# One of three attention stages rebuilt: two heads a step in the halves of TensorE's array, V stationary, branches summed in PSUM

## The chip, the cores and the metric

The kernel runs on one core of one Trainium2 chip. The metric is the device time of one launch in microseconds; smaller is better.

## The reference

Three transformer-like blocks in a row over 512 tokens of width 1024, all in float32. The third block holds the part that matters here, an attention of 16 heads of 64 with four groups of keys and values (four heads share one), in three branches whose outputs are summed with gates:

```python
# q: 16 heads; k_cmp/v_cmp, k_slc/v_slc, k_win/v_win: 4 groups; gates: sigmoid, 3 per head
y = g0 * attend(q, k_cmp, v_cmp) + g1 * attend(q, k_slc, v_slc) + g2 * attend(q, k_win, v_win)
mixed = merge[0] * (y_diff @ w_proj_diff) + merge[1] * (y @ w_proj_nsa)
```

The compressed branch has 31 keys, 32 in the kernel. At 512 tokens the selected and the window branch are both plain causal attention over all earlier keys, each with its own keys and values. Each row of scores gets its own maximum, exponential and sum.

## The kernel before

The program is a list of 43 stages, run by all engines in the same order, with a barrier between stages (`barrier`, L276: every engine drains and adds one to a semaphore, and waits until all four have). A stage marked `AHEAD` lets TensorE skip that wait and go on. Weights stream in through two slots on SyncE's queue for the whole program; most stages are matmuls in three fp32r parts over them (L148 to L186). The stages here, in order:

`to_fm` (L1395, planned at L2075) turns queries and keys with TensorE transposes to feature-major form; ScalarE copies them out of PSUM, the queries to `QF` (16 heads, two in the 128 partitions of each of 8 slices), each half of the keys to the lower 64 rows of `KF` (L1412). GpSimd fills the upper 64 rows of `KF` and of `QZN` with zeros (L1788).

`cattn` (L1678 to L1774) computes the gates `GT` and the compressed branch: scores with 64-row matmuls (L1686), softmax scaled by its gate, transposes (L1695), values with `PTC` stationary and `VBD` moving (L1703), copies to `ON` (L1772).

`nsa` (L1793 to L1819) is the two causal branches, with the helpers that the other attention stages use too: `attn_pe`, `attn_act`, `attn_dve` (L1097 to L1154). A loop over four groups has 32 steps each: one head, one branch and one block of 128 queries a step. The step's scores are one matmul with the zero-padded queries stationary and (block + 1) x 128 keys moving (L1094) and a mask matmul in bf16 (L1095). VectorE takes the negated maximum (L1165), ScalarE the exponential with the row sum (L1160). Three steps later TensorE transposes the weights (L1112) and ScalarE copies them (L1136); one step after that TensorE multiplies them with V, the turned weights stationary, V moving 64 columns (L1121). After four steps VectorE divides by the sum, applies the gate and adds to `ON` (L1808 to L1817). Scores have four PSUM banks, turned weights two, outputs two. A group starts with ScalarE copying four heads to `QZN` (L1264).

`split_fm` (L1286) turns `ON` to feature-major form and splits it in two fp32r parts, `YNH` (L1300) and `YNL` (L1306). `merge` (L1830 to L1875) projects both attentions; its first matmul of a pass waits for `mg.free`, which VectorE raises at the start of its part of the stage (L1856).

Engines run their instructions in order. Nothing but the text of the functions sets the order in the attention stages.

Of the kernel before, what the change touches and what calls it, by code (L numbers as in the profile page):

```python
# [23 lines left out]
ALU = mybir.AluOpType  # L24
# [3 lines left out]
P = 128  # L28
# [15 lines left out]
NSA_G = 4  # L44
# [6 lines left out]
def build(nc, A, out):  # L51
# [1104 lines left out]
    def one_softmax(act, dve, PBx):  # L1156
# [393 lines left out]
    ON = a_("ON", 0, [P, NC_, DM])  # L1550
    nq, nkv = turn(left_s, left=8), turn(left_s, left=12)


# [120 lines left out]
    PTC = a_("PTC", 72, [P, 2, SEQ])  # L1674
    GFM = PTC[:, 0, :]
    ca = sems("ca", "gate sig mask sc m ex p tr pt o od")

    def cattn_pe(pe):  # L1678
        narrow_pe(pe, nr[2], 6, SW[1], 0, 48, GFM).then_inc(ca.gate, 1)
        pe.wait_ge(ca.sig, 1)  # L1680
        for g in range(NSA_G):
            for r in range(2):
                half = slice(r * HD, (r + 1) * HD)
                for k in range(2 * NC_):
                    qb, j = divmod(k, 2)
# [3 lines left out]
        for g in range(NSA_G + 1):
            if g < NSA_G:  # L1690
                pe.wait_ge(ca.p, g + 1)
                if g >= 2:
                    pe.wait_ge(ca.pt, g - 1)
                for qb in range(NC_):
                    last = pe.transpose(PS[:, g % 2, qb * P:(qb + 1) * P], T3[:, g, qb * P:(qb + 1) * P], IDF[:, :])  # L1695
                last.then_inc(ca.tr, 1)
            if g:
                q = g - 1
                pe.wait_ge(ca.pt, q + 1)
                if q >= 2:  # L1700
                    pe.wait_ge(ca.od, q - 1)
                for qb in range(NC_):
                    last = pe.matmul(PS[:, 2 + 2 * (q % 2) + qb // 2, (qb % 2) * 256:(qb % 2) * 256 + 256],  # L1703
                                     PTC[:, q % 2, qb * P:(qb + 1) * P], VBD[:, q, :], start=True, stop=True)
                last.then_inc(ca.o, 1)

    def cattn_act(act):
        act.wait_ge(ca.gate, 1)
        act.activation(GT[:, :, :], PS[:, 7, 0:192].rearrange("p (c k) -> p c k", c=NC_), ACT.Sigmoid)
        act.drain().then_inc(ca.sig, 1)  # L1710
        for g in range(NSA_G):
            act.wait_ge(ca.m, g + 1)
            act.activation(SC[g], SC[g], ACT.Exp).then_inc(ca.ex, 1)
        for g in range(NSA_G):
            act.wait_ge(ca.tr, g + 1)
            if g >= 2:
                act.wait_ge(ca.o, g - 1)
            act.activation(PTC[:, g % 2, :], PS[:, g % 2, :], ACT.Copy).then_inc(ca.pt, 1)
# [10 lines left out]
    def cattn_dve(dve):  # L1729
# [39 lines left out]
        for g in range(NSA_G):  # L1769
            dve.wait_ge(ca.o, g + 1)  # L1770
            for b in range(2):
                dve.tensor_copy(ON[:, 2 * b:2 * b + 2, g * 256:(g + 1) * 256],  # L1772
                                PS[:, 2 + 2 * (g % 2) + b, :].rearrange("p (a k) -> p a k", a=2))
            dve.drain().then_inc(ca.od, 1)  # L1774

    QZN = a_("QZN", 76, [P, HPG, SEQ])
    PTN = a_("PTN", 72, [P, 2, SEQ])
    OTMP = a_("OTMP", 84, [P, NC_, HD])  # L1780
    NSTEP = HPG * 2 * NC_
    na = attn_turn(NSA_G, NSTEP, 4)

    def pn(t, a, b):

        return T3[:, t % NP, a:b]

    def zero_rows(pool):  # L1788

        for T in (KF[0], KF[1], QZN):  # L1790
            pool.memset(T[HD:P, :, :], 0.0)

    def nsa_pe(pe):  # L1793
        attn_pe(pe, na, NSA_G, NSTEP, 4,
                lambda g, t: scores_pe(pe, t % 4, QZN[:, t // 8, (t % 4) * P:(t % 4 + 1) * P],
                                       lambda n: flat(KF[t // 4 % 2][:, ds(g, 1), 0:n]), t % 4),
                lambda k, b: pn(k, b * P, (b + 1) * P), PTN,
                lambda g, k, b: T3[:, b, ds(768 + 512 * (k // 4 % 2) + HD * g, HD)], (na.ex, na.at.ex + 4 + 1), HD)

    def nsa_act(act):  # L1800
        exps, _ = one_softmax(act, None, pn)
        attn_act(act, na, NSA_G, NSTEP, 4, lambda g: head_queries(act, QZN, QF, g), exps, PTN)

    def nsa_dve(dve):
        def output(g, q):
            hh, branch = q // 2, q % 2
            inv, rw = (RW[:, 8 * (q % 2) + r:8 * (q % 2) + r + 4] for r in (0, 4))
            dve.reciprocal(inv, RS[:, 4 * (q % 4):4 * (q % 4) + 4])  # L1808
            dve.drain()
            dve.tensor_tensor(rw.unsqueeze(2), inv.unsqueeze(2),  # L1810
                              GT[:, :, ds(12 * g + 3 * hh + 1 + branch, 1)], ALU.mult)
            dve.drain()
            dve.tensor_tensor(OTMP[:, :, :], PS[:, 6 + q % 2, 0:256].rearrange("p (c d) -> p c d", c=NC_),
                              rw.unsqueeze(2).to_broadcast([P, NC_, HD]), ALU.mult)
            dve.drain()
            o = ON[:, :, ds(g * 256 + hh * HD, HD)]
            return dve.tensor_tensor(o, o, OTMP[:, :, :], ALU.add)  # L1817
# [201 lines left out]
    def stages(e, kind):  # L2019

        fns = STAGES[kind]
        for k, fn in enumerate(fns):
            if fn is not None:
# [148 lines left out]
```

## Time and profile before

| | |
|---|---|
| median of 3 runs | 3137.61 us (3129.13 to 3139.46) |
| the profiled execution | span 3135.7 us, first to last instruction |
| TensorE busy | 2773.3 us, 88% |
| VectorE, ScalarE, GpSimd busy | 1427.0, 1149.6, 35.4 us |
| TensorE's mean granted clock | 0.933 of 2.4 GHz |

Times are microseconds from the span's start. PE is TensorE's matmuls, PEld its weight loads, DVE is VectorE, ACT ScalarE, POOL GpSimd. PEclk is the granted clock as a share of 2.4 GHz; 0.50 is 1.2 GHz. Ends of matmuls are modelled, so starts are the firmer numbers.

### The profile page before, as it was taken

The page shows a single profiled execution, that of the slowest core. Times are in us where ns is not written, and L with a number is a line of the kernel's source. Part 1 is how long each engine was busy: PE and PEld are TensorE (multiplying, and loading weights), DVE is VectorE, ACT ScalarE, POOL GpSimd, SP SyncE. Part 2 cuts the span into 40 slices and gives each one's busy share as a digit, 9 for nine tenths or more (in the row PEclk, how much of TensorE's full clock was granted, in tenths as well). Part 3 has the DMA queues.
Part 4 walks back from the last instruction along what each step waited for, and adds up shares of the span by engine and source line. Part 5 has one row for each costly group of instructions (what it writes and reads, how often), then busy time and mean ns, then how long its engine had stood idle before and what let it go on. Part 6 is the DMA issues. An engine that isn't in the chain of part 4 may idle for free. (4 is left out here: it accounts for less than half of the span.)

```text
span 3135.7 us, 37199 instructions
## 1 busy us (share of the span) xinstructions
PE 2773.3 (88%) x12589; PEld 2174.5 (69%) x12589; DVE 1427.0 (46%) x2122; ACT 1149.6 (37%) x1965; POOL 35.4 (1%) x86
## 2 busy tenths in 40 slices
PE   7994879899997989889999796887489999899998
PEld 5872658588784867668877575676467788677776
DVE  3465232677524223367732476664444433252332
ACT  2241231455313346255521424433256633242231
POOL 0000000000001000000000000000100000000000
PEclk8997779999998999999999898998599999999999
DMA  3330002133221310123322121131000033222332
GB/s 110 96 95 6 27 27 94 54 94 100 94 94 34 94 54 0 54 67 94 100 94 87 44 88 34 45 96 54 4 1 0 0 94 97 78 74 94 87 94 81
DMA packets 270183, 206.36 MB, mean 66 GB/s; under 512 B 12004, under 2 KB 225681, under 8 KB 270113
## 3 DMA queue, kind: packets, MB, share of 16 engines
q1 hardware_dynamic: 258384, 197.16, 20.6%
q10 hardware_dynamic: 11729, 8.28, 0.8%
q8 instruction: 42, 0.69, 0.1%
q14 instruction: 28, 0.23, 0.0%
HBM read 203.28 MB, written 2.10 MB: 65 GB/s over the span
## 5 line engine op out<-in xcount | busy, mean ns | idle before, releaser
L146 DVE TENSOR_TENSOR WL<-RAW,WH 128x1024 fp32r<-128x1024 f32 x370 | 453.2, 1225 | 1021.7 <-ACT WH L141 1016.7
L141 ACT ACTIVATE WH<-RAW 128x1024 fp32r<-128x1024 f32 x370 | 391.7, 1059 | 1073.8 <-PE PS L155 864.7
L153 PE MATMUL PS<-XH,WH 128*128 128x512 f32 x1504 | 595.0, 396 | 56.8 <-DVE XL L593 28.3
L154 PE MATMUL PS<-XL,WH 128*128 128x512 f32 x1504 | 590.5, 393 | 0.0
L155 PE MATMUL PS<-XH,WL 128*128 128x512 f32 x1504 | 590.0, 392 | 0.0
L153 PEld LDWEIGHTS PS<-XH,WH 128*128 128x128 f32 x1504 | 285.2, 190 | 131.8 <-issue 49.0
L155 PEld LDWEIGHTS PS<-XH,WL 128*128 128x128 f32 x1504 | 285.4, 190 | 60.2
L154 PEld LDWEIGHTS PS<-XL,WH 128*128 128x128 f32 x1504 | 285.8, 190 | 57.7
L150 PE MATMUL PS<-WH,XH 128*128 128x512 f32 x480 | 199.0, 414 | 18.4 <-DVE WL L146 8.5
L151 PE MATMUL PS<-WH,XL 128*128 128x512 f32 x480 | 196.0, 408 | 0.0
L152 PE MATMUL PS<-WL,XH 128*128 128x512 f32 x480 | 195.3, 407 | 0.0
L1165 DVE TENSOR_REDUCE NM<-PS 128x1 f32<-128x128 f32 x192 | 93.4, 490 | 149.6 <-PE PS L1095 149.5
L153 PE MATMUL PS<-FH,WH 128*128 (+1 forms) x352 | 139.1, 395 | 3.3 <-ACT UP L691 3.3
L155 PE MATMUL PS<-FH,WL 128*128 (+1 forms) x352 | 138.9, 395 | 0.0
L154 PE MATMUL PS<-FL,WH 128*128 (+1 forms) x352 | 138.9, 395 | 0.0
L150 PEld LDWEIGHTS PS<-WH,XH 128*128 128x128 f32 x480 | 96.5, 201 | 43.6 <-DVE WL L146 11.8
L152 PEld LDWEIGHTS PS<-WL,XH 128*128 128x128 f32 x480 | 95.5, 199 | 21.2
L151 PEld LDWEIGHTS PS<-WH,XL 128*128 128x128 f32 x480 | 96.0, 200 | 20.2
L153 PE MATMUL PS<-MH,WH 128*128 (+1 forms) x256 | 101.3, 396 | 3.3 <-ACT RL L1906 3.3
L155 PE MATMUL PS<-MH,WL 128*128 (+1 forms) x256 | 101.1, 395 | 0.0
L154 PE MATMUL PS<-ML,WH 128*128 (+1 forms) x256 | 101.1, 395 | 0.0
L1121 PE MATMUL PS<-T,PTN 128*128 x640 | 87.0, 267 | 1.9 <-ACT PTN L1136 0.7
(431 smaller groups left out, 4059.6 us busy)
## 6 DMA issues: line engine op xcount, KB each, us to landing
RAW<-in_ffn_w_up SPq DMA_DIRECT2D x88, 512.0 KB, 3.7
RAW<-in_w_in SPq DMA_DIRECT2D x60, 512.0 KB, 3.5
RAW<-in_sc_ssm_w_in SPq DMA_DIRECT2D x44, 512.0 KB, 3.6
RAW<-in_ffn_w_down SPq DMA_DIRECT2D x44, 512.0 KB, 3.5
RAW<-in_w_mlp_up SPq DMA_DIRECT2D x32, 512.0 KB, 4.0
RAW<-in_w_mlp_down SPq DMA_DIRECT2D x32, 512.0 KB, 3.6
RAW<-in_fox_w_in SPq DMA_DIRECT2D x24, 512.0 KB, 3.7
RAW<-in_sc_ssm_w_out SPq DMA_DIRECT2D x16, 512.0 KB, 3.6
```

What stands on the lines that cost most here:

```text
L141: act.activation(WH[:, slot, :], RAW[:, slot, :], ACT.Copy).then_inc(hi_ready, 1)
L146: dve.tensor_tensor(WL[:, slot, :], RAW[:, slot, :], WH[:, slot, :], ALU.subtract).then_inc(lo_ready, 1)
L150: pe.matmul(o, ah, wh, start=first, stop=False)
L151: pe.matmul(o, al, wh, start=False, stop=False)
L152: return pe.matmul(o, ah, wl, start=False, stop=last)
L153: pe.matmul(o, wh, ah, start=first, stop=False)
L154: pe.matmul(o, wh, al, start=False, stop=False)
L155: return pe.matmul(o, wl, ah, start=False, stop=last)
L1121: last = pe.matmul(PS[:, 6 + k // NC_ % 2, o], PTx[:, k % 2, b * P:(b + 1) * P], value(i, k, b), start=b == 0, stop=b == k % 4)
L1165: return dve.tensor_reduce(NM[:, t % 4:t % 4 + 1], PS[:, t % 4, 0:w], AX, ALU.max, negate=True)
```

## The change

The attention stage gets helpers of its own. A step `t` of 16 is one pair of heads in one branch, with all four blocks of queries; heads are read in place from `QF`, partitions 0 to 63 and 64 to 127, and the keys are kept twice, once in each half of the partitions. Scores come in three parts (`SUBS`): block 3; blocks 2 and 0; block 1. They have two pairs of PSUM banks. The weights are normalised and gated by GpSimd before they are turned, in five chunks through two banks. Values have V stationary (64 columns) and the turned weights moving, so the output is feature-major already; the two branches and the compressed one add up in one PSUM bank. A stage `ysplit` then only splits `QF` in two parts.

```diff
+    SUBS = (((3, 0),), ((2, 0), (0, 384)), ((1, 0),))
+    CHUNKS = (((0, 0, 0),), ((0, 1, 0), (0, 3, 384)), ((1, 0, 0),), ((1, 1, 0), (1, 3, 384)),
+              ((0, 2, 0), (1, 2, 256)))
...
+    def pair_scores_pe(pe, s, t, sub, query, key, bias=None):
+        i = 3 * t + sub
+        if i >= 2:
+            pe.wait_ge(s.ex, s.at.ex + i - 1)
+        banks = [2 * (i % 2) + hh for hh in range(2)]
+        for hh in range(2):
+            for k, (qb, c0) in enumerate(SUBS[sub]):
+                d = c0 + qb * P
+                pe.matmul(PS[:, banks[hh], d:d + P], IDB[:, :], MROW[:, :], start=k == 0, stop=False,
+                          skip_group_check=True)
+        for qb, c0 in SUBS[sub]:
+            n = (qb + 1) * P
...
+            for hh in range(2):
+                last = pe.matmul(PS[:, banks[hh], c0:c0 + n], query(t, hh, qb), key(t, hh, n), start=False,
+                                 stop=True, skip_group_check=True)
+        last.then_inc(s.sc, 1)
+
+    def pair_turn_pe(pe, s, t, chunk, Px):
+        j = 5 * t + chunk
+        if chunk == 0:
+            pe.wait_ge(s.nr, s.at.nr + 3 * t + 3)
+        if j >= 2:
+            before = chunk - 2 if chunk >= 2 else chunk + 3
+            done = t if chunk >= 2 else t - 1
+            if before in (0, 2):
+                pe.wait_ge(s.pa, s.at.pa + 2 * done + before // 2 + 1)
+            else:
+                pe.wait_ge(s.pd, s.at.pd + 3 * done + {1: 1, 3: 2, 4: 3}[before])
...
+    def pair_values_pe(pe, s, t, o, opens, PTx, value):
+        pe.wait_ge(s.pa, s.at.pa + 2 * t + 2)
+        pe.wait_ge(s.pd, s.at.pd + 3 * t + 3)
+        for b in range(NC_):
+            for hh in range(2):
+                last = pe.matmul(PS[64 * hh:64 * hh + 64, 6 + o % 2, b * P:SEQ], value(t, hh, b), pt_of(PTx, hh, b),
+                                 start=opens and b == 0, stop=b == NC_ - 1, skip_group_check=True)
+        last.then_inc(s.pv, 1)
+
+    def pair_pe(pe, s, n, Px, PTx, query, key, value, bias=None, first_values=None, per_out=1):
+        for t in range(n + 2):
+            if t < n:
+                pe.wait_ge(s.qk, s.at.qk + t // per_out + 1)
+                pair_scores_pe(pe, s, t, 0, query, key, bias)
+            if t >= 2:
+                k = t - 2
+                o = k // per_out
+                if k % per_out == 0 and o >= 2:
+                    pe.wait_ge(s.od, s.at.od + o - 1)
+                if k % per_out == 0 and first_values is not None:
+                    first_values(pe, o)
+                pair_values_pe(pe, s, k, o, k % per_out == 0 and first_values is None, PTx, value)
+            if t < n:
+                pair_scores_pe(pe, s, t, 1, query, key, bias)
+            if 1 <= t <= n:
+                for chunk in range(3):
+                    pair_turn_pe(pe, s, t - 1, chunk, Px)
+            if t < n:
+                pair_scores_pe(pe, s, t, 2, query, key, bias)
+            if 1 <= t <= n:
+                for chunk in range(3, 5):
+                    pair_turn_pe(pe, s, t - 1, chunk, Px)
...
+    def pair_act(act, s, n, Px, PTx, output, per_out=1):
+        for t in range(n + 2):
+            if t < n:
+                pair_exps_act(act, s, t, 0, Px)
+                pair_exps_act(act, s, t, 1, Px)
+            if t >= 2 and (t - 2) % per_out == per_out - 1:
+                act.wait_ge(s.pv, s.at.pv + t - 1)
+                output((t - 2) // per_out).then_inc(s.oa, 1)
+            if 1 <= t <= n:
+                for chunk in (0, 2):
+                    act.activation(*pair_copy(act, s, t - 1, chunk, PTx), ACT.Copy).then_inc(s.pa, 1)
+            if t < n:
+                pair_exps_act(act, s, t, 2, Px)
...
+    def pair_dve(dve, s, n, PTx, output, per_out=1):
+        for t in range(n + 2):
+            if t < n:
+                pair_maxima_dve(dve, s, t, 0)
+            if 1 <= t <= n:
+                pair_weights_dve(dve, s, t - 1, 2)
+            if t < n:
+                pair_maxima_dve(dve, s, t, 1)
+                pair_weights_dve(dve, s, t, 0)
+            if t >= 2 and (t - 2) % per_out == per_out - 1:
+                o = (t - 2) // per_out
+                dve.wait_ge(s.oa, s.at.oa + o + 1)
+                output(o).then_inc(s.od, 1)
+            if 1 <= t <= n:
+                dve.tensor_copy(*pair_copy(dve, s, t - 1, 1, PTx)).then_inc(s.pd, 1)
+            if t < n:
+                pair_maxima_dve(dve, s, t, 2)
+                pair_weights_dve(dve, s, t, 1)
+            if 1 <= t <= n:
+                for chunk in (3, 4):
+                    dve.tensor_copy(*pair_copy(dve, s, t - 1, chunk, PTx)).then_inc(s.pd, 1)
+
+    def pair_pool(pool, s, n, Px, gate=None):
...
+                for qb, _ in SUBS[sub]:
+                    for hh in range(2):
+                        col = 8 * (t % 2) + NMCOL[qb] + hh
+                        p = Px[:, t % 2, hh, POFF[qb]:POFF[qb] + (qb + 1) * P]
+                        pool.tensor_scalar(p, p, RW[:, col:col + 1], 1.0 if gate is None else gate(t, hh, qb),
+                                           ALU.mult, ALU.mult)
+                pool.drain().then_inc(s.nr, 1)
...
                     for h, d in enumerate(dst):
-                        last = act.activation(d[0:HD, :], PS[h * HD:(h + 1) * HD, k % 4, :], ACT.Copy)
+                        for to in range(2):
+                            last = act.activation(d[to * HD:(to + 1) * HD, :], PS[h * HD:(h + 1) * HD, k % 4, :], ACT.Copy)
...
     def cattn_pool(pool):
+        for b in range(2):
+            pool.tensor_copy(VN[b][:, :, :], T3[:, :, 768 + 512 * b:1024 + 512 * b])
...
+        def compressed(pe, o):
+            pe.matmul(PS[:, 6 + o % 2, :], VBD[:, o // 2, (o % 2) * P:(o % 2 + 1) * P], PTC[:, o // 2, :],
+                      start=True, stop=False, skip_group_check=True)
+        pair_pe(pe, na, 2 * NPAIR, PN, PTN, query, key, value, None, compressed, 2)
...
+    def ysplit_act(act):
+        for j in range(KT):
+            act.activation(YNH[:, j, :], QF[:, j, :], ACT.Copy).then_inc(ny.hi, 1)
+
+    def ysplit_dve(dve):
+        for j in range(KT):
+            dve.wait_ge(ny.hi, j + 1)
+            dve.tensor_tensor(YNL[:, j, :], QF[:, j, :], YNH[:, j, :], ALU.subtract).then_inc(ny.lo, 1)
...
                 ah, al = ((YDH, YDL), (YNH, YNL), (XH, XL), (XH, XL))[u % 4]
+                if isinstance(i, int) and u == 1:
+                    pe.wait_ge(ny.lo, KT)
                 unit_fm(pe, first["merge"], 8, i, u, PS[:, u, :], ah, al)
-        loop(pe, "merge", body)
+        loop(pe, "merge", body, peel=1)
...
-              pool_too=zero_rows),
+              ),
         (cattn_pe, cattn_act, cattn_dve, cattn_pool),
-        (nsa_pe, nsa_act, nsa_dve, None),
-        split_fm(ON, YNH, YNL),
+        (nsa_pe, nsa_act, nsa_dve, nsa_pool),
+        (None, ysplit_act, ysplit_dve, None, AHEAD),
```

Not shown: `cattn` loses its values (L1703), its copies to `ON` (L1772) and the waits between them; the old bodies of `nsa_pe`, `nsa_act`, `nsa_dve` and `zero_rows` go; tiles move in SBUF. `pair_weights_dve` is one reciprocal of the sums for each part of the scores. The output copy of `pair_act` writes `QF`; that of `pair_dve` is a drain. The other two attention stages are as they were.

## Rows read from the trace of the kernel before

**Rows 1.** The page's first line.

```profile
span 3135.7 us, 37199 instructions
```

**Rows 2.** Stretches of attention and split; busy time (instructions) by engine, PEclk, DMA, GB/s.

```profile
2290.00:2492.40 202.40, 191.95 (x1344) 151.83 (x1344) 96.20 (x256) 136.94 (x400) 0.00 (x0) 0.97 0.00 0
2492.40:2500.40 8.00, 5.73 (x33) 5.26 (x34) 5.16 (x9) 4.67 (x9) 0.00 (x0) 0.79 0.01 2
```

**Rows 3.** Timeline of one head and branch; start, duration, engine, line, count, idle before.

```profile
2353.06 0.44 PE L1094 MATMUL PS<-KSF,QZN 128*128 x2
...
2355.81 0.61 PE L1112 MATMUL PS<-IDF,T 128*128 128x128 f32 x4
...
2356.26 0.78 PE L1121 MATMUL PS<-T,PTN 128*128 x6
...
2356.87 1.08 PE L1094 MATMUL PS<-KSF,QZN 128*128 x2
...
2357.79 0.22 PE L1095 MATMUL PS<-MROW,IDB 128*128 128x128 bf16 x1
...
2357.96 1.00 PE L1121 MATMUL PS<-T,PTN 128*128 x8
2358.04 0.69 DVE L1165 TENSOR_REDUCE NM<-PS 128x1 f32<-128x512 f32 x1 [1.47 <-PE PS L1095]
...
2358.80 0.44 PE L1094 MATMUL PS<-KWF,QZN 128*128 x2
...
2359.07 0.22 PE L1095 MATMUL PS<-MROW,IDB 128*128 128x128 bf16 x1
```

**Rows 4.** Groups of 2226 to 2290 us, the 64-row matmuls; busy, mean ns.

```profile
L1686 PE MATMUL PS<-KCF,QF 64*128 64x32 f32 x128 | 20.7, 389 | 1.8 <-ACTq L1710 1.8
```

**Rows 5.** Groups of the attention stage by form; busy, mean ns, idle before.

```profile
L1136 ACT ACTIVATE PTN<-PS 128x512 f32<-128x512 f32 x32 | 19.1, 597 | 11.5 <-PE PS L1112 11.5
L1160 ACT ACTIVATE T<-PS,NM 128x384 f32<-128x384 f32 x32 | 18.4, 575 | 2.8 <-DVE NM L1165 2.8
L1165 DVE TENSOR_REDUCE NM<-PS 128x1 f32<-128x384 f32 x32 | 17.8, 557 | 14.6 <-PE PS L1095 14.6
...
L1160 ACT ACTIVATE T<-PS,NM 128x128 f32<-128x128 f32 x32 | 11.6, 363 | 4.5 <-DVE NM L1165 4.5
...
L1165 DVE TENSOR_REDUCE NM<-PS 128x1 f32<-128x128 f32 x32 | 9.3, 290 | 19.7 <-PE PS L1095 19.7
```

**Rows 6.** GpSimd's groups over the whole span.

```profile
L1322 POOL TENSOR_TENSOR RABQ<-TABD,BCP 128x64 f32<-128x64 f32 x4 | 1.3, 322 | 811.4 <-ACTq L278 811.4
...
L1725 POOL TENSOR_SCALAR_AFFINE_SELECT T<-T 128x128 f32<-128x128 f32 x1 | 0.3, 308 | 0.2 <-POOLq L1722 0.2
```

**Rows 7.** Stretches around three falls of the granted clock; columns as in rows 2.

```profile
2233.70:2236.80 3.10, 0.00 (x0) 0.00 (x0) 0.00 (x0) 3.00 (x6) 0.00 (x0) 0.96 0.00 0
2236.80:2243.80 7.00, 6.23 (x16) 2.98 (x17) 0.00 (x0) 0.67 (x2) 0.52 (x2) 0.53 0.00 0
2288.40:2291.60 3.20, 0.00 (x0) 0.00 (x0) 1.22 (x2) 1.50 (x3) 0.00 (x0) 0.94 0.00 0
2291.60:2298.00 6.40, 5.23 (x13) 2.80 (x14) 1.27 (x3) 2.71 (x8) 0.00 (x0) 0.50 0.01 3
1970.20:1973.90 3.70, 1.66 (x12) 1.39 (x12) 3.28 (x8) 2.14 (x6) 0.00 (x0) 0.98 0.00 0
1973.90:1977.10 3.20, 3.20 (x15) 2.90 (x14) 0.00 (x0) 2.84 (x5) 0.00 (x0) 0.50 0.00 0
```

**Rows 8.** Groups of 2226 to 2290 us, half of the key copies of `to_fm`.

```profile
L1412 ACT ACTIVATE KWF<-PS 64x512 f32<-64x512 f32 x4 | 2.4, 592 | 0.1
```

**Rows 9.** Timeline, the end of `cattn`.

```profile
2277.00 3.12 DVE L1767 TENSOR_TENSOR T<-T,TINY 128x512 f32<-128x512 f32 x4
...
2288.33 1.29 DVE L1772 COPY ON<-PS 128x512 f32<-128x512 f32 x2 [0.44 <-PE PS L1703]
```

**Rows 10.** The merge's subtractions; count, ns min/median/max, first and last start.

```profile
L1872 DVE TENSOR_TENSOR MXL<-MT,MXH x8: 691/691/693, 2528.2 to 2682.5; 128x512 f32 x8
```

More of the change, by code:

```diff
@@ L1166, in one_softmax, with pt_of @@
         return exps, maxima
+    SUBS = (((3, 0),), ((2, 0), (0, 384)), ((1, 0),))
+    POFF = (0, 128, 384, 768)
+    NMCOL = {3: 0, 0: 2, 2: 4, 1: 6}
+    CHUNKS = (((0, 0, 0),), ((0, 1, 0), (0, 3, 384)), ((1, 0, 0),), ((1, 1, 0), (1, 3, 384)),
+              ((0, 2, 0), (1, 2, 256)))
+    PTAT = {0: (0, 0), 1: (1, 0), 3: (1, 384)}
+    def pt_of(PTx, hh, b):
+        n = SEQ - b * P
+        if b == 2:
+            return PTx[:, 4, 256 * hh:256 * hh + n]
+        chunk, at = PTAT[b]
+        return PTx[:, 2 * hh + chunk, at:at + n]
@@ new lines, in build, with pair_turn @@
+    pair_s = shared("pair", "qk sc mx ex rw nr tr pa pd pv oa od")
+    def pair_turn(n, per_out=1):
+        return turn(pair_s, qk=n // per_out, sc=3 * n, mx=3 * n, ex=3 * n, rw=3 * n, nr=3 * n, tr=5 * n, pa=2 * n,
+                    pd=3 * n, pv=n, oa=n // per_out, od=n // per_out)
+    def pair_scores_pe(pe, s, t, sub, query, key, bias=None):
[10 more added lines that the diff above has]
+            n = (qb + 1) * P
+            if bias is not None:
+                for hh in range(2):
+                    pe.matmul(PS[:, banks[hh], c0:c0 + n], *bias(t, hh, n), start=False, stop=False,
+                              skip_group_check=True)
+            for hh in range(2):
+                last = pe.matmul(PS[:, banks[hh], c0:c0 + n], query(t, hh, qb), key(t, hh, n), start=False,
+                                 stop=True, skip_group_check=True)
+        last.then_inc(s.sc, 1)
@@ new lines, in pair_turn_pe @@
+    def pair_turn_pe(pe, s, t, chunk, Px):
[9 more added lines that the diff above has]
+                pe.wait_ge(s.pd, s.at.pd + 3 * done + {1: 1, 3: 2, 4: 3}[before])
+        for hh, b, at in CHUNKS[chunk]:
+            for qb in range(b, NC_):
+                c = at + (qb - b) * P
+                last = pe.transpose(PS[:, 4 + j % 2, c:c + P], Px[:, t % 2, hh, POFF[qb] + b * P:POFF[qb] + (b + 1) * P],
+                                    IDF[:, :])
+        last.then_inc(s.tr, 1)
@@ new lines, in pair_exps_act @@
+    def pair_exps_act(act, s, t, sub, Px):
+        i = 3 * t + sub
+        act.wait_ge(s.mx, s.at.mx + i + 1)
+        if sub == 0 and t >= 2:
+            act.wait_ge(s.tr, s.at.tr + 5 * (t - 2) + 5)
+        for qb, c0 in SUBS[sub]:
+            n = (qb + 1) * P
+            for hh in range(2):
+                col = 8 * (t % 2) + NMCOL[qb] + hh
+                last = act.activation(Px[:, t % 2, hh, POFF[qb]:POFF[qb] + n], PS[:, 2 * (i % 2) + hh, c0:c0 + n],
+                                      ACT.Exp, bias=NM[:, col:col + 1], accum_out=RS[:, col:col + 1])
+        last.then_inc(s.ex, 1)
@@ new lines, in pair_maxima_dve, with pair_weights_dve @@
+    def pair_maxima_dve(dve, s, t, sub):
+        i = 3 * t + sub
+        dve.wait_ge(s.sc, s.at.sc + i + 1)
+        for qb, c0 in SUBS[sub]:
+            n = (qb + 1) * P
+            for hh in range(2):
+                col = 8 * (t % 2) + NMCOL[qb] + hh
+                last = dve.tensor_reduce(NM[:, col:col + 1], PS[:, 2 * (i % 2) + hh, c0:c0 + n], AX, ALU.max, negate=True)
+        last.then_inc(s.mx, 1)
+    def pair_weights_dve(dve, s, t, sub):
+        i = 3 * t + sub
+        dve.wait_ge(s.ex, s.at.ex + i + 1)
+        if t >= 2:
+            dve.wait_ge(s.nr, s.at.nr + i - 5)
+        c0, w = ((0, 2), (2, 4), (6, 2))[sub]
+        c0 += 8 * (t % 2)
+        dve.reciprocal(RW[:, c0:c0 + w], RS[:, c0:c0 + w]).then_inc(s.rw, 1)
@@ new lines, in pair_pool @@
+    def pair_pool(pool, s, n, Px, gate=None):
+        for t in range(n):
+            for sub in range(3):
+                pool.wait_ge(s.rw, s.at.rw + 3 * t + sub + 1)
+                for qb, _ in SUBS[sub]:
+                    for hh in range(2):
+                        col = 8 * (t % 2) + NMCOL[qb] + hh
+                        p = Px[:, t % 2, hh, POFF[qb]:POFF[qb] + (qb + 1) * P]
+                        pool.tensor_scalar(p, p, RW[:, col:col + 1], 1.0 if gate is None else gate(t, hh, qb),
+                                           ALU.mult, ALU.mult)
+                pool.drain().then_inc(s.nr, 1)
@@ L1549, in build @@
     RABKS, RABKW = a_("RABKS", 56, [P, NC_, 2, HD]), a_("RABKW", 58, [P, NC_, 2, HD])
-    ON = a_("ON", 0, [P, NC_, DM])
     nq, nkv = turn(left_s, left=8), turn(left_s, left=12)
@@ L1673, in build @@
     CMASK = T3[:, 0, 512:512 + P].rearrange("p (c n) -> p c n", c=NC_)
-    PTC = a_("PTC", 72, [P, 2, SEQ])
+    PTC = a_("PTC", 72, [P, NSA_G, SEQ])
     GFM = PTC[:, 0, :]
-    ca = sems("ca", "gate sig mask sc m ex p tr pt o od")
+    ca = sems("ca", "gate sig mask sc m ex p tr pt")
     def cattn_pe(pe):
@@ L1688, in cattn_pe @@
             last.then_inc(ca.sc, 1)
[L1689 to L1705, printed above, removed]
+        for g in range(NSA_G):
+            pe.wait_ge(ca.p, g + 1)
+            if g >= 2:
+                pe.wait_ge(ca.pt, g - 1)
+            for qb in range(NC_):
+                last = pe.transpose(PS[:, g % 2, qb * P:(qb + 1) * P], T3[:, g, qb * P:(qb + 1) * P], IDF[:, :])
+            last.then_inc(ca.tr, 1)
     def cattn_act(act):
@@ L1768, in cattn_dve @@
             dve.drain().then_inc(ca.p, 1)
[L1769 to L1791, printed above, removed]
-    def nsa_pe(pe):
[L1794 to L1798, printed above, removed]
+    PN = a_("PN", 16, [P, 2, 2, 1280])
@@ new lines, in build, with query, key, value @@
+    PTN = a_("PTN", 4, [P, 5, SEQ])
+    NPAIR = HEADS // 2
+    na = pair_turn(2 * NPAIR, 2)
+    def nsa_pe(pe):
+        def query(t, hh, qb):
+            return QF[HD * hh:HD * hh + HD, t // 2, qb * P:(qb + 1) * P]
+        def key(t, hh, n):
+            return KD[t % 2][HD * hh:HD * hh + HD, t // 4, 0:n]
+        def value(t, hh, b):
+            return VN[t % 2][:, b, HD * (t // 4):HD * (t // 4 + 1)]
+        def compressed(pe, o):
+            pe.matmul(PS[:, 6 + o % 2, :], VBD[:, o // 2, (o % 2) * P:(o % 2 + 1) * P], PTC[:, o // 2, :],
+                      start=True, stop=False, skip_group_check=True)
+        pair_pe(pe, na, 2 * NPAIR, PN, PTN, query, key, value, None, compressed, 2)
@@ L1800, in nsa_act @@
     def nsa_act(act):
-        exps, _ = one_softmax(act, None, pn)
-        attn_act(act, na, NSA_G, NSTEP, 4, lambda g: head_queries(act, QZN, QF, g), exps, PTN)
+        act.drain().then_inc(na.qk, NPAIR)
+        pair_act(act, na, 2 * NPAIR, PN, PTN, lambda o: act.activation(QF[:, o, :], PS[:, 6 + o % 2, :], ACT.Copy), 2)
     def nsa_dve(dve):
[L1805 to L1817, printed above, removed]
@@ L1818, in nsa_dve, with nsa_pool, gate @@
-        _, maxima = one_softmax(None, dve, None)
-        attn_dve(dve, na, NSA_G, NSTEP, maxima, output)
+        pair_dve(dve, na, 2 * NPAIR, PTN, lambda o: dve.drain(), 2)
+    def nsa_pool(pool):
+        def gate(t, hh, qb):
+            col = 3 * (2 * (t // 2) + hh) + 1 + t % 2
+            return GT[:, qb, col:col + 1]
+        pair_pool(pool, na, 2 * NPAIR, PN, gate)
+    ny = sems("ny", "hi lo")
+    def ysplit_act(act):
+        for j in range(KT):
+            act.activation(YNH[:, j, :], QF[:, j, :], ACT.Copy).then_inc(ny.hi, 1)
@@ L2076, in build @@
               + [(lambda c, b=b, j=j: T3[:, c, 512 + 512 * b + j * P:512 + 512 * b + (j + 1) * P],
-                  (KF[b][:, 2 * j, :], KF[b][:, 2 * j + 1, :]), 1.0) for b in range(2) for j in range(2)],
-              pool_too=zero_rows),
+                  (KD[b][:, 2 * j, :], KD[b][:, 2 * j + 1, :]), 1.0) for b in range(2) for j in range(2)],
+              ),
         (cattn_pe, cattn_act, cattn_dve, cattn_pool),
-        (nsa_pe, nsa_act, nsa_dve, None),
-        split_fm(ON, YNH, YNL),
+        (nsa_pe, nsa_act, nsa_dve, nsa_pool),
+        (None, ysplit_act, ysplit_dve, None, AHEAD),
         (merge_pe, merge_act, merge_dve, None),
```

18 lines of the change are left out of this document (11 added, 7 removed).

## The prediction

> **What bounds the kernel now.** I read four views, from coarse to fine: the page's span, the table of stages by windows, the groups of the attention stage, and its timeline. The span is 3135.7 us, 1.9 below the median of 3137.61 [rows 1]; the sum is made against the span, and 1.9 is added at the end. All that the change touches lies between 2226 and 2500 us, and the attention stage is 202.4 us of it, with TensorE busy 192.0, VectorE 96.2 and ScalarE 136.9 [rows 2]. TensorE is the bound there, and the timeline shows why: one head and branch (four query blocks) repeats every 5.74 us, 2353.06 to 2358.80 [rows 3], while the others wait for it. 32 of these are 184 us; the rest is four loop starts and drains.
>
> TensorE's prices are starts minus starts [rows 3]: a score matmul of 512 keys 0.92 (2356.87 to 2357.79) in two passes, of 128 keys 0.27, so 1.7 ns a column, 0.49 and 0.70 for 256 and 384; a mask matmul 0.055; four transposes 0.45; values of four blocks, P turned stationary and V moving, 0.84. A head and branch is 2.38 + 0.22 + 1.1 + 2.1 = 5.8, the period. Two of them, the work of one new step, take **11.5 us**.
>
> **The change, part by part.** A step is now a pair of heads in one branch; 16 steps, unrolled.
>
> *TensorE's work.* Scores: the same eight matmuls with 64 rows each, two heads in the two row halves. Masks and 20 transposes stay, 0.44 and 2.2. Values: V stationary in 64 columns, P moving, 1280 columns a head, in the two column halves: 2.38 a head, like the scores, against 4.2 for both heads before. A branch-free term of 0.92 every second step is the compressed branch. How far two halves overlap is the first unknown. The one row with 64-row matmuls runs eight of one half, then eight of the other [rows 4], so it tells nothing of it. Bounds: full overlap halves scores and values, none leaves 4.8 and 4.8. Each f32 matmul is two passes (x2 in the rows), and I assume that passes start in the order of issue: the second pass of head 0 waits for its first, and head 1 stands behind it. So one pass overlaps the neighbour's and a lone pair takes three passes instead of two or four. I take that, the middle: S0 (512 keys, both heads, masks) 1.46, S1 (384 and 128) 1.47, S2 (256) 0.82, values 2.7. By work alone a step is 9.8 us, below 11.5.
>
> *The order on the engines.* This decides. In a step TensorE issues S0, values of two steps ago, S1, turn 0, 1, 2 of the last step, S2, turn 3, 4. Turn 2 reuses the bank of turn 0, so it waits for copy 0; ScalarE issues copy 0 behind the exponentials of S1, these wait for VectorE's maxima of S1, and these for S1. Behind turn 2, S2, turns 3 and 4, the next S0 and the values all queue. From the end of S1 I follow the chain. Result and wake-up 0.2 (a record of 1.08 where the next starts after 0.92, and a maximum that starts 0.03 behind the mask [rows 3]). Maxima of 384 and 128 for two heads, 2 x (0.557 + 0.290) less 0.2 of overlap, 1.5; exponentials 2 x (0.575 + 0.363) plus hand-over, 1.9 [rows 5]. The output copy 0.6 every second step, 0.3; copy 0, 0.6 [rows 5]; wake-ups 0.1; turn 2, 0.45. That is 5.0, of which TensorE can fill 0.9 with turns 0 and 1; some 3.5 us it stands idle. Then S2 0.82, turns 3 and 4 0.9, S0 1.46, compressed 0.46 on the mean, values 2.7, S1 1.47: **12.8 us**. The values also wait for copy 4 on VectorE: S2 end + 0.2 + maxima 0.8 (256 columns lie between the two rows of 5, at 0.42) + reciprocal 0.2 + two copies 1.3, which falls together with the end of S0 and costs nothing now; with faster scores it would be next.
>
> *GpSimd* now multiplies the weights by gate over sum, 2560 columns a step, which the trace has never shown. Nearest rows: affine-select of 128 columns 0.31, or 2.4 ns a column and 6.2 us a step; tensor-tensor of 64 columns 0.32, 5 ns and 12.9 us [rows 6]. The first is nearest in width. What waits for it is turn 0, on the last 512 columns: released at about S0's end + 1.7, they take 1.2 (2.6 at the other end), and turn 0 is wanted 4.6 after S0's end. Hidden at both ends by itself; at the high end the engine's 12.9 us would just reach the period.
>
> *Array mode.* Six times a step the array goes between full, row-halved and column-halved matmuls. The trace shows no switch. Lower bound 0; upper 0.16 each, the lag by which a result trails its stream [rows 3]; a gain is excluded, since a switch issues nothing. I take 0.4 a step of at most 1.0. The Trainium skill, "TensorEngine Tiling (Array Packing)", Key Properties, says that changing the mode (not just the tile) drains the engine. That speaks for the upper end, some 9 us more over the stage; no run here shows it yet.
>
> *TensorE's clock.* Before, the attention stage has almost no idle time, and the clock is 0.97 of 2.4 GHz [rows 2]. Two idle stretches of 3.1 and 3.2 us were each followed by 1.2 GHz, for 7.0 and 6.4 us, 6.2 and 5.2 of them busy; after 3.7 us that were 1.7 busy it was 3.2 us [rows 7]. The new step idles 3.5 us in one piece. One fall a step at the shortest of these, 3.2 us at half speed, costs 1.6; the longest would cost 3.1; none costs 0. I take 1.6.
>
> A step is then 12.8 + 0.4 + 1.6 = **14.8 us**. Start: S0, S1, maxima, exponentials until bank 0 is free again, S0, S1 of the second step, 9.4 us; 14 periods, 207.2; the end, 5.8 through S2, then turns 0.9, compressed and values until 10.9, turns and copies of the last step 4.4, values 2.7, output 0.6: 18.6, with 2 for the clock 20.6. Together 237.2 against 202.4 [rows 2]: **+34.8**.
>
> *The other edits.* Eight more key copies on ScalarE, last in their stage, 2.42 for four [rows 8]: +4.8. GpSimd's zero-filling there goes, and its V copies come before the compressed mask: off the path, the mask being wanted 10 us later. Compressed values leave their stage: its last scaling ended at 2280.1, then one turn and copy end it at 2281.7, not 2289.6 [rows 9]: -7.9. The split stage was 7.9 (nearly all of its stretch [rows 2]): its transposes go, but TensorE's head start into the merge is none, since the first merge matmul waits for `mg.free`, which VectorE gives only behind its eight subtractions and the barrier: 0.6 + 8 x 0.69 [rows 10] + 0.4 = 6.5, -1.4. Sum of these -4.5.
>
> Total +30.3: span 3166, median **3168**.
>
> **Rivals.**
> *The array overlaps fully* and keeps its clock. S0 1.03, S1 1.2, S2 0.6, values 2.4, bound by copy 4: a step 11.7 + 0.4. Stage 9 + 14 x 12.1 + 17.5 = 196; with -4.5 the total is -11, 3127, faster. It decides below a step of 12.8. For it: the prices of passes; against it: the order of passes, and the idle 3.5 us that no overlap removes. The Trainium skill, same page, Theoretical Speedup, gives up to 2x for 64 rows. With the clock's fall it is 13.7 a step, 3152, slower.
> *Overlap in part, clock held*: 13.2 a step, stage 213, total +6: 3144, within the bound.
> *No overlap*: S0 1.95, S1 2.2, S2 1.1, values 4.8: 16.3 + 0.2 + 1.6 = 18.1; stage 288, total +81: 3219. That is also the case in which the change doesn't do what it says.
> *GpSimd becomes the bound* at over 14.8 us a step: +15 per us, from 3168 up.
>
> **Numbers.** About 0.3% (9.4 us) is what a measurement of this kernel can tell from no change. Partial overlap with falls 0.42, with the clock held 0.12; full overlap with falls 0.15, clock held 0.10; none 0.17; GpSimd 0.04. Faster 0.12. Same 0.15, the case at 3144 and the low edge of 3152. Slower 0.73. The range runs from 3130, which leaves out most of the full overlap at clock, to 3214, which leaves out half of no overlap.
>
> **What would show it.** In the changed trace: one TensorE gap of 3.1 to 3.6 us in each of 16 steps, ended by a ScalarE copy, before turn 2; the granted clock of the stage well under 0.97; a period of 14 to 15.5; scores of a pair of 512 keys in 1.4 us. A period at or under 12.8 would prove me wrong; a score pair of 1.9 us would mean no overlap; a gap that GpSimd ends before turn 0, the last rival.

## The result and the profile after

| | before | after |
|---|---|---|
| median | 3137.61 us | 3153.43 us (3148.17 to 3153.84) |
| ratio after to before | | 1.0048, 95% interval 1.0034 to 1.0061 |
| profiled execution, span | 3135.7 us | 3152.0 us |
| TensorE busy, mean granted clock | 2773.3 us, 0.933 | 2741.0 us, 0.923 |
| GpSimd busy | 35.4 us | 108.8 us |

The kernel became slower by 15.8 us, 0.5%. I had forecast slower, but by 30, and 3153 stands inside my range; so the sign and the mechanism held and a size was off by half.

The page of the changed kernel: TensorE is busy for 32 us less, and the kernel is slower all the same.

```profile
span 3152.0 us, 35829 instructions
PE 2741.0 (87%) x12157; PEld 2115.2 (67%) x12157; DVE 1417.8 (45%) x2082; ACT 1110.1 (35%) x1869; POOL 108.8 (3%) x213
```

Stretches, to set against [rows 2]: the attention stage, then the first 3.5 us of the merge behind it (columns as there: length, busy time and count of PE, PEld, DVE, ACT, POOL, PEclk, DMA, GB/s).

```profile
2286.45:2508.45 222.00, 169.98 (x976) 100.93 (x976) 91.62 (x224) 91.84 (x296) 76.69 (x128) 0.86 0.00 1
2514.50:2518.00 3.50, 3.47 (x8) 2.82 (x9) 0.00 (x0) 1.28 (x1) 0.00 (x0) 0.50 0.00 0
```

The stage takes 222.0 us instead of 202.4, with TensorE busy 170 instead of 192 and the clock at 0.86 instead of 0.97. What TensorE waited for in the stage (us, times, longest), longest first:

```profile
PE PS L1228 <- ACT PTN L1294: 47.5, 17, 3.4
PE PS L1201 <- ACT PN L1274: 2.7, 2, 1.7
...
PE PS L1228 <- POOLq L1349: 0.2, 1, 0.2
```

One wait holds nearly all of it: a turn (L1228) that waits for ScalarE's copy (L1294), once in each step from the second on, 3.44 us with an output copy and 2.95 without (2.30 the first time). GpSimd was waited for once, 0.2 us. The timeline of one long step, from the end of scores part 1 to the next:

```profile
2380.68 1.09 PE L1228 MATMUL PS<-IDF,PN 128*128 128x128 f32 x8
2380.80 1.42 DVE L1305 TENSOR_REDUCE NM<-PS 128x1 f32<-128x384 f32 x4 [2.34 <-PE PS L1210]
...
2382.26 0.58 ACT L1274 ACTIVATE PN<-PS,NM 128x384 f32<-128x384 f32 x1 [2.38 <-DVE NM L1305]
...
2384.07 0.61 ACT L1968 ACTIVATE QF<-PS 128x512 f32<-128x512 f32 x1
2384.55 0.62 ACT L1294 ACTIVATE PTN<-PS 128x512 f32<-128x512 f32 x1
...
2385.22 0.66 PE L1228 MATMUL PS<-IDF,PN 128*128 128x128 f32 x4 [3.44 <-ACT PTN L1294]
...
2385.91 1.17 PE L1210 MATMUL PS<-KWD,QF 64*128 64x256 f32 x4
...
2387.02 1.97 PE L1228 MATMUL PS<-IDF,PN 128*128 128x128 f32 x8
...
2389.12 1.25 PE L1210 MATMUL PS<-KSD,QF 64*128 64x512 f32 x4
...
2390.31 1.13 PE L1962 MATMUL PS<-PTC,VBD 128*128 128x512 f32 x2
...
2391.37 2.38 PE L1237 MATMUL PS<-PTN,VSN 128*64 128x512 f32 x16
...
2393.67 0.40 PE L1201 MATMUL PS<-MROW,IDB 128*128 128x128 bf16 x4
...
2394.00 1.14 PE L1210 MATMUL PS<-KSD,QF 64*128 64x384 f32 x8
...
2395.07 1.09 PE L1228 MATMUL PS<-IDF,PN 128*128 128x128 f32 x8
```

Turns 0 and 1, then maxima, exponentials, output copy, copy 0, and turn 2 only behind 3.44 us of idle TensorE: the chain as the prediction has it. Turns 3 and 4, eight transposes, take 1.76 us (2387.02 to 2388.78), against 0.93 in the filler run below at full clock: the granted clock has fallen under them. The idle stretch of this step, and the stretch behind turn 2 (columns as above):

```profile
2381.80:2385.20 3.40, 0.00 (x0) 0.00 (x0) 0.81 (x5) 2.91 (x10) 1.52 (x2) 1.00 0.01 2
2386.10:2389.40 3.30, 3.30 (x16) 2.39 (x18) 1.92 (x5) 1.43 (x5) 1.33 (x3) 0.50 0.00 0
```

Steps alternate 14.4 us and 12.8 us. Counted from VectorE's maxima of scores part 1, the second step and the last, 14 periods apart, give the mean, (2489.66 - 2299.65) / 14 = **13.57 us**:

```profile
2299.65 1.42 DVE L1305 TENSOR_REDUCE NM<-PS 128x1 f32<-128x384 f32 x4 [1.19 <-PE PS L1210]
...
2489.66 1.42 DVE L1305 TENSOR_REDUCE NM<-PS 128x1 f32<-128x384 f32 x4 [2.34 <-PE PS L1210]
```

Outside the stage, to set against [rows 8] and [rows 9]: twice eight key copies instead of twice four (KWD from 2236.7 to 2241.6), +4.9; the compressed stage 44.8 instead of 52.5 us, -7.7; from the end of the attention to the first merge matmul 6.1 instead of 7.9, -1.8; and the merge's first unit runs at 1.2 GHz for 3.5 us and more (second row above), +2.1, which I had not counted. With +19.6 of the stage that is +17.1; the stretch ahead of these stages was 0.7 shorter in this execution, which leaves 16.4, and the spans differ by 16.3.

### The profile page after: what moved, and what is told of

The parts are those of the page before. It is cut to its first block and busy times, and to the rows that moved or that the text cites. A ratio compares the mean times of both kernels' runs of the same rounds, so it can differ in the third digit from the quotient of the medians.

```text
span 3152.0 us, 35829 instructions
## 1 busy us (share of the span) xinstructions
PE 2741.0 (87%) x12157; PEld 2115.2 (67%) x12157; DVE 1417.8 (45%) x2082; ACT 1110.1 (35%) x1869; POOL 108.8 (3%) x213
## 5 line engine op out<-in xcount | busy, mean ns | idle before, releaser
L1274 ACT ACTIVATE PN<-PS,NM 128x512 f32<-128x512 f32 (+3 forms) x128 | 66.1, 525 | 109.3 <-DVE NM L1305 109.3
L1228 PE MATMUL PS<-IDF,PN 128*128 128x128 f32 x320 | 59.3, 339 | 47.6 <-ACT PTN L1294 47.5
```

The source lines that it names most:

```text
L1228: last = pe.transpose(PS[:, 4 + j % 2, c:c + P], Px[:, t % 2, hh, POFF[qb] + b * P:POFF[qb] + (b + 1) * P], IDF[:, :])
L1274: last = act.activation(Px[:, t % 2, hh, POFF[qb]:POFF[qb] + n], PS[:, 2 * (i % 2) + hh, c0:c0 + n], ACT.Exp, bias=NM[:, col:col + 1], acc ...
```

## The experiments

The profiled executions differ by up to 11 us in where the attention stage begins (2278.2 to 2289.1), upstream of every edit here, so beside each median (in us; the kernel before ran beside them at 3137.7 and 3138.2) I give the mean step, from the same row of VectorE as above over 14 periods.

| run | median | step |
|---|---|---|
| changed kernel | 3153.4 | 13.57 |
| copy 0 ahead | 3111.6 | 11.06 |
| filler in the gap | 3128.1 | 12.06 |
| values head by head | 3180.2 | 15.37 |
| mg.free ahead | 3148.5 | 13.59 |
| combined | 3092.5 | 10.05 |
| GpSimd twice | 3159.1 | 13.83 |
| more switches | 3174.5 | 14.69 |

### Copy 0 ahead of the exponentials

```diff
                 pair_exps_act(act, s, t, 0, Px)
+            if 1 <= t <= n:
+                act.activation(*pair_copy(act, s, t - 1, 0, PTx), ACT.Copy).then_inc(s.pa, 1)
+            if t < n:
                 pair_exps_act(act, s, t, 1, Px)
...
-                for chunk in (0, 2):
-                    act.activation(*pair_copy(act, s, t - 1, chunk, PTx), ACT.Copy).then_inc(s.pa, 1)
+                act.activation(*pair_copy(act, s, t - 1, 2, PTx), ACT.Copy).then_inc(s.pa, 1)
```

> Edit: ScalarE issues copy 0 of the last step ahead of the exponentials of scores part 1, instead of behind them; nothing else. Theory (the order on ScalarE holds TensorE 2.9 or 3.4 us in every step, and this idle stretch also brings the clock down): the gap before turn 2 shrinks from 3.4 to under 1 us; the next wait in line is the output copy that VectorE waits for, and copy 4. By the rows of the changed kernel I get 9.9 us for a step without output and 10.9 with it, 10.6 with some loss, instead of 13.57; 3 us by 16 steps is 47 us, so about 3106 us against 3153, which is also below the 3137 of the kernel before. Rival A (TensorE's own work with its mode switches is the bound, and the gap only shows slack): the step stays over 12.8. Rival B (GpSimd, which multiplies before the turns, takes the place): TensorE's gap moves to before turn 0, and the step stays near 12 to 13.

Measured 3111.6 us, 0.9926 (0.9900 to 0.9951) of the kernel before, and a step of 11.06. One instruction moved past four, and in every second step past the output copy too, took 42 us off (47 were expected) and made the changed kernel faster than the one before. TensorE's waits in the stage:

```profile
PE PS L1228 <- DVE PTN L1333: 15.4, 7, 2.2
PE PS L1228 <- ACT PTN L1296: 5.5, 9, 0.7
PE PS L1228 <- ACT PTN L1289: 4.0, 16, 0.3
```

The 47.5 us for copy 0 are now 4.0 (L1289). Rival A falls. Rival B too: TensorE waited once for GpSimd, 0.2 us. Next in line is what was expected: VectorE's copy 1, behind its wait for the output copy, in every second step. A part of the gain is the clock, 0.94 instead of 0.86.

### Filler in the gap

```diff
-                for chunk in range(3):
+                for chunk in range(2):
                     pair_turn_pe(pe, s, t - 1, chunk, Px)
+                if t < n:
+                    pe.wait_ge(s.ex, s.at.ex + 3 * t + 1)
+                    for _ in range(3):
+                        pe.matmul(PS[:, 2 * (t % 2), :], IDF[:, :], PTC[:, 0, :], start=True, stop=True,
+                                  skip_group_check=True)
+                pair_turn_pe(pe, s, t - 1, 2, Px)
```

> Edit: in TensorE's gap of 2.9 or 3.4 us before turn 2 three f32 matmuls of 512 columns (0.85 us each) write into the bank that the scores of part 2 overwrite next; work for nothing, the output stays the reference's. Theory (the idle stretch brings the clock to 1.2 GHz for 3.4 us in each step, under turns 3 and 4 and the scores of part 2): the granted clock of the stage goes from 0.86 to over 0.97, and a step falls from 13.57 by 1.2 to about 12.4 us, 18 us in all, 3135. Rival (the clock's falls lie where other engines are waited for anyway): the clock rises but the time stays within 3 us. If the filler itself delays turn 2, the step grows by up to 0.3.

Measured 3128.1 us, 25 below the changed kernel where 18 were expected, and 0.9976 (0.9964 to 0.9989) of the kernel before. Busy and clock of the stage and of its 14 steps, the same steps of the changed kernel, and TensorE's longest waits:

```profile
2286.00:2488.00 202.00, 187.90 (x1075) 103.75 (x1074) 89.08 (x225) 92.98 (x299) 76.20 (x128) 0.96 0.00 1
2302.46:2471.36 168.90, 160.93 (x939) 89.24 (x940) 77.07 (x197) 79.90 (x260) 66.68 (x112) 1.00 0.00 1
```

```profile
2299.65:2489.66 190.01, 146.29 (x855) 88.26 (x856) 80.00 (x197) 80.00 (x260) 67.11 (x113) 0.87 0.00 1
```

```profile
PE PS L1228 <- ACT PTN L1300: 9.0, 16, 0.9
PE PS L1201 <- ACT PN L1280: 2.7, 2, 2.1
```

The chain is as long as before (turn 0 to the masks behind turn 2 takes 4.53 us in a step without output copy, in both kernels) and every engine does the same useful work; only TensorE computes nothing of use for 2.6 us a step, and a step falls from 13.57 to (2471.36 - 2302.46) / 14 = 12.06:

```profile
2302.46 1.42 DVE L1311 TENSOR_REDUCE NM<-PS 128x1 f32<-128x384 f32 x4 [1.19 <-PE PS L1210]
...
2471.36 1.42 DVE L1311 TENSOR_REDUCE NM<-PS 128x1 f32<-128x384 f32 x4 [2.43 <-PE PS L1210]
```

The rival falls. So the idle stretch costs twice: itself, and 1.5 us a step for the half clock behind it.

### Values head by head

```diff
-        for b in range(NC_):
-            for hh in range(2):
+        for hh in range(2):
+            for b in range(NC_):
```

> Edit: the eight value matmuls of a step are issued all of one head, then all of the other, so neighbours lie in the same column half and only one pair in the middle can overlap. Theory (values of two heads run at the same time in the two column halves, 2.3 us instead of 4.6): values take 4.3 to 4.5 us, they are in the chain, so a step grows by 2.1 and the run by 33 us to 3187. Rival (the overlap is worth less, since the values end before something else that is waited for): under 10 us.

Measured 3180.2 us, +27 where +33 was expected; a step +1.8. The values of one step, and what follows them:

```profile
2368.89 3.93 PE L1237 MATMUL PS<-PTN,VSN 128*64 128x512 f32 x16
2372.75 0.40 PE L1201 MATMUL PS<-MROW,IDB 128*128 128x128 bf16 x4
```

They take 3.86 us, not the 4.3 to 4.5 expected, and 2.30 in the changed kernel (2391.37 to 2393.67). The two halves do overlap, and in full when neighbours alternate: a head's 1280 columns in two passes are 2.13 us of stream (two cycles of 2.4 GHz a column and pass, as 0.427 us from one 512-column pass to the next in the trace). That 3.86 is less than twice 2.13 has its reason in this view of the first 1.6 us, the matmuls running in it by shape (L1962 is the end of the compressed term):

```profile
L1237 PE MATMUL PS<-PTN,VSN 128*64 128x512 f32 x3 | 1.7, 626 | 0.0
L1237 PE MATMUL PS<-PTN,VSN 128*64 128x384 f32 x2 | 0.8, 486 | 0.0
L1962 PE MATMUL PS<-PTC,VBD 128*128 128x512 f32 x1 | 0.6, 592 | 0.0
L1237 PE MATMUL PS<-PTN,VSN 128*64 128x256 f32 x1 | 0.4, 379 | 0.0
```

Three passes of 512 columns have started when only one of 256 has. Each head has two of 512, so the third is the other head's first, and by the program it comes behind both passes of 256 and both of 128 of this head. It started ahead of three passes that were issued before it, in the other half of the array.

The trace of the kernel before shows the same, in the stretch that [rows 4] was taken to say nothing of. In the compressed scores, 16 passes of one half are issued, then 16 of the other. Matmuls running in two neighbouring stretches, at 1.2 GHz both (busy PE and count, PEld and count, PEclk):

```profile
2254.85:2255.70 0.85, 0.85 (x6) 0.85 (x5) 0.50 0.00 0
2255.70:2256.55 0.85, 0.85 (x10) 0.85 (x9) 0.50 0.00 0
```

Alone, a pass starts 0.213 us after the last; from 2255.78 on two rows of starts run side by side, 6 to 27 ns apart, and each 16 passes take 2.59 us instead of 3.41. Here too the first pass of the other half starts ahead of three that were issued before it. That engines run their instructions in order, as the description of the kernel has it, does not hold for TensorE's matmuls in different halves.

### mg.free ahead

```diff
     def merge_dve(dve):
-        dve.drain().then_inc(mg.free, 2)
...
     def ysplit_dve(dve):
+        dve.drain().then_inc(mg.free, 2)
         for j in range(KT):
```

> Edit: VectorE raises mg.free at the start of its subtractions in ysplit instead of behind them and the barrier. Theory (this semaphore takes away TensorE's head start into the merge): the first merge matmul starts some 0.5 us after the attention's end instead of 6.1 us, the first unit of 24 matmuls (5.5 us, or more at 1.2 GHz) runs beside the split, and 4 to 6 us go: 3148. Rival (TensorE then waits for ny.lo or for the weights instead): 0 to 1 us.

Measured 3148.5, 5 us less, the step the same. The medians alone hardly tell this: 1.0036 (1.0022 to 1.0050) of the kernel before, against 1.0048 (1.0034 to 1.0061) for the changed one. The trace does. TensorE's wait before the merge is 1.0 instead of 6.7 us:

```profile
PE PS L153 <- DVEq L1986: 1.0, 1, 1.0
```

and from the first split copy to the first use of `YNH` pass 5.9 us (2510.7 to 2516.6) instead of 13.7: the idle stretch is gone and with it the merge's start at half clock (its first matmuls start 0.23 us apart, not 0.43). The reading of this semaphore was right.

### Combined

```diff
+            if 1 <= t <= n:
+                act.activation(*pair_copy(act, s, t - 1, 2, PTx), ACT.Copy).then_inc(s.pa, 1)
             if t >= 2 and (t - 2) % per_out == per_out - 1:
                 act.wait_ge(s.pv, s.at.pv + t - 1)
                 output((t - 2) // per_out).then_inc(s.oa, 1)
...
                     dve.tensor_copy(*pair_copy(dve, s, t - 1, chunk, PTx)).then_inc(s.pd, 1)
+            if t >= 2 and (t - 2) % per_out == per_out - 1:
+                o = (t - 2) // per_out
+                dve.wait_ge(s.oa, s.at.oa + o + 1)
+                output(o).then_inc(s.od, 1)
```

> Edit: copy 0 ahead of the exponentials of part 1 (as in e1), the output copy behind copy 2 on ScalarE and VectorE's wait for it behind its last copy, and mg.free ahead (as in e4). In the trace of e1 every second step still has a gap of 2.2 us before turn 3, ended by VectorE's copy 1, which stands behind its wait for the output copy. Theory (all three are waits of the order of issue, independent of each other): these gaps shrink to under 0.7, 8 x 1.7 = 14 us, and the merge starts 5 us earlier, so 3111.6 - 19 = 3093 us. Rival (the output copy is then late for TensorE, which waits for its PSUM bank before the compressed values): the gap moves there and only the 5 us of the merge are won, 3107.

Measured **3092.5 us**, 3093 expected, 0.9854 (0.9838 to 0.9871) of the kernel before, 61 us under the changed one, with not one operation more or less. The stage is 169 us at a clock of 0.97, and TensorE's waits for these copies 0.9 us a step:

```profile
2282.50:2451.50 169.00, 150.43 (x976) 85.19 (x976) 90.48 (x224) 89.87 (x296) 76.21 (x128) 0.97 0.00 1
```

```profile
PE PS L1228 <- ACT PTN L1293: 10.4, 16, 0.7
PE PS L1228 <- ACT PTN L1289: 3.8, 15, 0.3
```

### GpSimd twice

```diff
                                            ALU.mult, ALU.mult)
+                pool.drain()
+                for qb, _ in SUBS[sub]:
+                    for hh in range(2):
+                        p = Px[:, t % 2, hh, POFF[qb]:POFF[qb] + (qb + 1) * P]
+                        pool.tensor_scalar(p, p, ONES[:, 0:1], ONES[:, 1:2], ALU.mult, ALU.mult)
                 pool.drain().then_inc(s.nr, 1)
```

> Edit: after gating, GpSimd multiplies each block of weights a second time by one, so it has 9.7 us of work in a step instead of 4.8; the output stays the reference's. Theory (GpSimd is hidden: its last two multiplications of a step end 2 us before TensorE could use them): no more than 3 us over the changed kernel's 3153. Rival (GpSimd or its share of SBUF holds VectorE and so the chain): 1 us a step or more, over 3169.

Measured 3159.1, 5.6 over the changed kernel, a step +0.26: more than the 3 expected, far less than the 16 of the rival. The ratios to the kernel before, 1.0072 (1.0055 to 1.0089) and 1.0048 (1.0034 to 1.0061), overlap, so the step and the waits decide. TensorE's waits:

```profile
PE PS L1228 <- ACT PTN L1294: 36.5, 15, 3.0
PE PS L1228 <- POOLq L1354: 14.0, 11, 3.9
```

With 9.7 us of work in a step GpSimd begins to hold turn 0, and most of that comes off the wait for copy 0 behind it. With its own 4.8 it is hidden.

### More switches

```diff
         for b in range(NC_):
+            if b:
+                pe.matmul(PS[:, 4 + (5 * t + 5) % 2, 0:P], IDB[:, :], MROW[:, :], start=True, stop=True,
+                          skip_group_check=True)
             for hh in range(2):
```

> Edit: a full-array bf16 matmul of 128 columns stands between the value matmuls of each two blocks, into a free bank, three a step; so the array changes between full and column-halved six more times. Theory (each change costs 0.10 us, as the starts in the trace show after a stream's end): 3 x 0.055 + 6 x 0.10 = 0.75 us a step, in the chain, so 12 us over the changed kernel: 3165. Rival (a change is free, only the stream counts): 0.17 a step, 3 us: 3156.

Measured 3174.5, +21, a step +1.12: even more than the 12 of the theory; the free switch falls. The values of one step:

```profile
2376.30 1.08 PE L1240 MATMUL PS<-PTN,VWN 128*64 128x512 f32 x4
2377.31 0.23 PE L1237 MATMUL PS<-MROW,IDB 128*128 128x128 bf16 x1
2377.47 0.87 PE L1240 MATMUL PS<-PTN,VWN 128*64 128x384 f32 x4
...
2379.55 0.40 PE L1201 MATMUL PS<-MROW,IDB 128*128 128x128 bf16 x4
```

They last 3.25 us (2376.30 to 2379.55) instead of 2.30. Of the 0.95 the three streams are 0.165, which leaves 0.13 for each of six changes. 0.10 of this lies between the end of a stream and the next start: a mask of 0.055 holds the array 0.16, from 2377.31 to 2377.47. The rest is in the first pass behind a change, which takes 0.05 longer than the others. The rest of the +1.12 is not in the values. The granted clock of the 14 steps is 0.86 here and 0.87 in the changed kernel, which goes that way; no run separates it.

## Why the prediction was right in the main and wrong in size

**The bound.** Right: TensorE's work a step fell below the old 11.5 us, and the step grew all the same. (The 9.8 us given for that work is 9.1 by the prediction's own terms; nothing hangs on it.) Busy TensorE went down by 22 us in a stage that grew by 20.

**The chain.** Right, and shown by the copy moved ahead. Forecast 5.0 us from the end of S1 through turn 2 on the mean, 5.3 in a step with an output copy and 4.7 in one without. From the last stream of S1 to the mask behind turn 2 it is 5.1 (2380.59 to 2385.71) and 4.6, so 0.1 less on the mean. The gap was forecast at 3.5 and is 3.44 and 2.95.

**Overlap of the halves: the step that failed.** "So one pass overlaps the neighbour's and a lone pair takes three passes instead of two or four. I take that, the middle". It rests on the sentence before it, that passes start in the order of issue. The head-by-head run shows that they don't when they lie in different halves, and the pairs run at full overlap. The combined run has whole steps at full clock; S0 with the compressed term behind it, and S1 with turn 0 behind it:

```profile
2361.12 1.13 PE L1210 MATMUL PS<-KSD,QF 64*128 64x512 f32 x4
2362.18 1.12 PE L1964 MATMUL PS<-PTC,VBD 128*128 128x512 f32 x2
...
2365.87 1.14 PE L1210 MATMUL PS<-KSD,QF 64*128 64x384 f32 x8
2366.94 1.09 PE L1228 MATMUL PS<-IDF,PN 128*128 128x128 f32 x8
```

Less the 0.10 of the array change behind each, S0 takes 0.96 us and not 1.35, S1 0.97 and not 1.25, S2 0.54 and not 0.71 (all without masks), the values 2.20 and not 2.7. The middle was 1.3 us a step too dear. The step was forecast at 14.8 and is 13.57, 1.2 less: the overlap is -1.3, the chain and the clock -0.1 each, the array changes +0.25. Over 14 periods that is -17. The start of the stage took 13.2 us and not 9.4, at a mean clock of 0.63 that the prediction had not counted, and its end 18.8 and not 20.6, so the stage missed by 15 and the whole by 14.

**Array modes.** Named, its size too small: 0.4 a step taken, with 1.0 as the end. The trace has eight changes in a step with the compressed term (into and out of each of three parts of scores, into the compressed term, into and out of the values) and seven in one without; the one behind S1 is hidden in the gap. Seven and six at 0.10 are 0.65 on the mean, some 0.85 at the 0.13 of the last run. The page "TensorEngine Tiling (Array Packing)" of the Trainium skill, Key Properties, says that such a change drains the engine; this case agrees in that each costs, 0.10 to 0.13 us.

**Clock.** Taken 1.6 a step, measured 1.5 by the filler (13.57 to 12.06). Right. That the merge, behind a stage with less work and an idle split, would begin at 1.2 GHz was missed: +2.1 us.

**GpSimd.** Hidden, as said, and cheaper than the lower of my two rows: 772 ns for 512 columns, 452 for 128, so 4.8 us a step and not 6.2.

**The other edits.** -4.6 without the merge's clock, forecast -4.5; each within 0.5.

**The rivals.** What happened is one of them, to which I gave 15%: full overlap with the clock's fall, 13.7 us a step and 3152 us; measured 13.57 and 3153. The "up to 2x" of the Trainium skill, "TensorEngine Tiling (Array Packing)", Theoretical Speedup, is borne out: the values of two heads take 2.30 us where the stream of one is 2.13.

**The signs.** Two held: one gap a step before turn 2, ended by a ScalarE copy (2.95 in each second step, a little under the 3.1 to 3.6 named), and a clock well under 0.97 (0.86). Two did not: the period, 13.57, lies under the 14 to 15.5 that was named, and the pair of 512 keys takes 1.06 us and not 1.4. Both say full overlap.

So the forecast of +30 is my sum with the wrong middle. Of two bounds far apart I took a mechanism of my own for the middle and gave it over half of the chance, though the trace of the kernel before had a stretch that spoke against it. The bounds were right.

## What to carry to other kernels

Less work on the engine that bounds a stage is not less time: when an order of issue is written by hand, follow one buffer's release across all engines and ask what stands ahead of it. Here one copy behind four exponentials cost 2.5 us a step, and its move turned +0.5% into -0.7%, with three more such moves -1.5%.

An idle stretch on TensorE can be paid again in the clock behind it: here 2.95 and 3.44 us of idleness in turn brought 1.5 us a step. Where such a stretch can't be filled, count the half clock behind it, into the next stage too.

An average row can hide what an assumption needs. The 128 matmuls of [rows 4] looked like one half after the other; their starts, one by one, showed both at once.

## What the runs showed of the hardware that I had not expected

Two f32 matmuls in different halves of the array run fully at once, passes included: values in 2.30 us where the stream of one head alone is 2.13. A matmul for the other half starts ahead of three passes issued before it, with column halves in the head-by-head run and with row halves in the kernel before.

Useless matmuls can pay: 2.6 us of filler a step saved 1.5 us a step, since the granted clock of the 14 steps was 1.00 instead of 0.87.

GpSimd's multiplication by two per-partition scalars in place costs 0.34 us and 0.83 ns a column (452 ns at 128, 772 at 512), and VectorE's rows beside it did not slow: with GpSimd's work doubled, its maxima of 384 and 128 columns took 553 and 280 ns on the mean, against 557 and 290 in the kernel before [rows 5], where GpSimd did nothing in that stage.
